# A two-block transformer kernel on one core: the feed-forward up projections in seven block products instead of eight, and one token product moved ahead of the attention logits

## The reference, cut to what matters

```python
def conv_ffn(hn, w_up, conv_w, conv_b, w_down):
    u = depthwise_conv_centred(hn @ w_up, conv_w, conv_b)     # 3 taps over the tokens
    gate, val = jnp.split(u, 2, axis=-1)
    return (jax.nn.gelu(gate, approximate=True) * val) @ w_down

def second_block(x, ...):
    for l in range(DEPTH_2):                                  # 2 layers
        mixed = hybrid_mixer(rms_norm(x, mix_pre_g[l]), ...)  # attention + mLSTM
        x = x + rms_norm(mixed, mix_post_g[l])
        ff = conv_ffn(rms_norm(x, ffn_pre_g[l]), w_up[l], ffn_conv_w[l], ffn_conv_b[l], w_down[l])
        x = x + rms_norm(ff, ffn_post_g[l])
    return x
```

## Time and profile before

| what | value |
|---|---|
| median of three executions | 2045.03 us (2043.11 to 2045.64) |
| the profiled execution: its time | 2044.89 us |
| the profiled execution: span of the trace | 2043.2 us |
| mean granted clock of TensorE | 0.989 of full speed |
| PE busy | 1953.8 us (96%), 9008 instructions |
| DVE busy | 652.7 us (32%) |
| ACT busy | 411.7 us (20%) |
| POOL busy | 110.3 us (5%) |

### The profile page before, as it was taken

The page is one execution under the profiler, slowest core; times in us unless marked ns, Lnnn a source line. Parts: engine busy times, 40 slices in busy tenths (PEclk is TensorE's granted clock), DMA queues, the critical chain, the costliest instruction groups (busy, mean ns, idle before and its releaser), DMA issues.

```text
span 2043.2 us, 23068 instructions
## 1 busy us (share of the span) xinstructions
PE 1953.8 (96%) x9008; PEld 1117.3 (55%) x9008; DVE 652.7 (32%) x1324; ACT 411.7 (20%) x871; POOL 110.3 (5%) x183
## 2 busy tenths in 40 slices
PE   7999999999989899989899999999999999999998
PEld 3767875333333233333333333756888456768863
DVE  1487513222112122211212221543333445433353
ACT  2134213111111011111101112143221023421210
POOL 0000000000000000000000000110000011000000
PEclk9999999999999999999999999999999999999999
DMA  9855368999999999999999999153544434344440
GB/s 344 295 202 191 131 231 333 418 427 428 428 427 428 428 428 427 428 428 427 428 428 428 427 426 369 62 206 114 174 137 164 147 131 165 113 135 154 136 173 33
DMA packets 136421, 582.21 MB, mean 285 GB/s; under 512 B 9848, under 2 KB 56064, under 8 KB 110752
## 3 DMA queue, kind: packets, MB, share of 16 engines
q1 hardware_dynamic: 131808, 574.70, 70.7%
q0 software_dynamic: 4544, 6.57, 1.1%
HBM read 580.18 MB, written 2.63 MB: 285 GB/s over the span
## 4 chain that ended last, share of the span: by engine, by line
PE 75%; DMA 20%; DVE 3%; ACT 1%; issue 1%; SPq 0%; DVEq 0%; ACTq 0%
PE psum L358 51%; DMA ring<-w_gu 11%; PE psum L694 11%; PE psum L636 9%; DMA work<-w_gu 9%; PE psum L2213 1%; DVE work L1854 1%; PE psum L681 1%; PE psum L670 1%; PE psum L1078 1%; DMA ring<-w_ada 0%; PE psum L1120 0%; PE psum L1109 0%; SPq L461 0%; DVE work L1852 0%
## 5 line engine op out<-in xcount | busy, mean ns | idle before, releaser
L358 PE MATMUL psum<-normed,ring 128*128 128x256 f32 (+1 forms) x2400 | 497.1, 368 | 0.0
L358 PEld LDWEIGHTS psum<-normed,ring 128*128 128x128 f32 x2400 | 434.4, 190 | 58.3 <-issue 4.1
L636 PE MATMUL psum<-ring,normed 128*64 128x512 f32 x1024 | 236.3, 615 | 33.0 <-DMA ring<-w_gu 31.8
L636 PE MATMUL psum<-work,normed 128*64 128x512 f32 x1024 | 234.3, 612 | 29.3 <-DMA work<-w_gu 29.3
L358 PE MATMUL psum<-work 128*128 128x128 f32 (+7 forms) x1248 | 227.3, 352 | 1.9 <-ACT work L2554 1.7
L358 PEld LDWEIGHTS psum<-work 128*128 128x128 f32 (+2 forms) x1248 | 151.7, 185 | 87.3 <-issue 74.3
L358 PE MATMUL psum<-ring,work 128*128 128x512 f32 (+1 forms) x464 | 197.5, 578 | 0.1
L636 PEld LDWEIGHTS psum<-ring,normed 128*64 128x64 f32 x1024 | 76.0, 141 | 190.9 <-issue 164.3
L636 PEld LDWEIGHTS psum<-work,normed 128*64 128x64 f32 x1024 | 80.5, 141 | 181.1 <-issue 181.1
L358 PE MATMUL psum<-ring,normed 128*128 128x512 f32 (+1 forms) x368 | 152.3, 567 | 0.7 <-PE psum L358 0.4
L358 PEld LDWEIGHTS psum<-ring,work 128*128 128x128 f32 x464 | 87.4, 190 | 100.0 <-issue 98.7
(11 more groups left out here) (328 smaller groups left out, 1425.0 us busy)
## 6 DMA issues: line engine op xcount, KB each, us to landing
ring<-w_gu SPq DMA_DIRECT2D x64, 2048.0 KB, 27.3
work<-w_gu SPq DMA_DIRECT2D x62, 2048.0 KB, 27.3
work<-w_dn SPq DMA_DIRECT2D x32, 2048.0 KB, 27.2
ring<-w_dn SPq DMA_DIRECT2D x28, 2048.0 KB, 27.5
ring<-w_in SPq DMA_DIRECT2D x23, 2048.0 KB, 10.1
ring<-w_up SPq DMA_DIRECT2D x44, 1024.0 KB, 7.2
ring<-w_down SPq DMA_DIRECT2D x10, 2048.0 KB, 7.8
ring<-w_ada SPq DMA_DIRECT2D x8, 2048.0 KB, 9.0
```

What stands on the lines that cost most here:

```text
L358: return pe.matmul(out, lhsT, rhs, start=first, stop=last, **kw)
L636: ins = pe.matmul(b[r], self.hgT[:, 2 * q + k, r], ws[e][:, k, n0:n0 + 512], start=q == 0 and k == 0, stop=q == QUARTERS - 1 and k == 1, s ...
```

## The change: what it does

1. **Seven products for eight in the up projections** (chunks 2 to 21 of both layers, `up_sevens`). For a chunk, the weights are seen as two parts (gate, value) by two halves of each pair of feature blocks, the tokens as two halves of each pair by two token tiles. Seven products of sums of these blocks, each summed over four pairs, replace the eight plain ones: 28 matmuls with 128 moving columns instead of 16 with 256. Four of the seven go to one PSUM bank (`up`), three to another (`upb`).
2. **Sums of the weights on POOL**: four instructions of 512 columns for every chunk (lines 2214 to 2217 of the changed kernel), the second of them written back into the ring slot. They wait for the chunk two places ahead to be done on the PE, since their results have two buffers.
3. **Sums of the tokens on DVE**: four instructions of 512 columns once a layer, behind the second tile's norm.
4. **Totals on DVE and ACT** for every chunk: ACT copies the first product out of PSUM (`first_product`, 128 columns), DVE makes four sums of one PSUM operand and one SBUF operand (`up_totals`, 256, 256, 128 and 256 columns), into a buffer `u_out` in SBUF. Both banks are released there. ACT's taps and DVE's outer taps then read `u_out` and no longer PSUM.
5. **The order on DVE and ACT is skewed**: in step c DVE does the totals of chunk c, the outer taps of c-1 and the product of c-2.
6. **The sums of hidden chunks** for the down projection move from POOL to DVE, behind steps 10 and 18.
7. **In the mixing stage**, PE's value product of tile 1 moves in front of the logits of tile 0, and the list of PSUM banks follows.

The core of the diff:

```diff
-    u += [("S", l, 0, g) for g in range(4)] + [("mv", l, 1)] + [("S", l, 1, g) for g in range(4)]
+    u += [("mv", l, 1)] + [("S", l, t, g) for t in range(NT) for g in range(4)]
...
-    u += [("up", l, c) for c in range(2, FC)]
+    u += [(name, l, c) for c in range(2, FC) for name in ("upb", "up")]
...
+    x_sums = Arena(mem.work, xn_at).take(4, KC // 2, P)
+    u_sums = [Arena(mem.work, at).take(4, P) for at in (aqk_at + 4096, aqk_at + 4608, hid_at + FC * L, ex_at + 1536, ex_at + 2048, ex_at + 2560)]
+    u_sums = [u_sums[0:3], u_sums[3:6]]
+    u_out = [hm.rearrange("p t h n -> p (t h) n"), mem.gain.rearrange("p (a b) -> p a b", b=P)]
...
+    def up_of(l, c, part):
+
+        if c < 2:
+            return bank("up", l, c)[:, part * L:(part + 1) * L]
+        return u_out[c % 2].rearrange("p a b -> p (a b)")[:, P + 4 * P * part:P + 4 * P * part + L]
...
-            for g in range(SEVENS // 4):
-                pool.wait_ge(hid_ready, l * FC + 8 * g + 8)
-                pairs = hid[:, 8 * g:8 * g + 8].rearrange("p (i k) t -> p i k t", k=2)
-                a11, a12, a21, a22 = (pairs[:, :, k, t * P:(t + 1) * P] for t in range(2) for k in range(2))
-                s1, s2, s3, s4 = (s_sums[:, i, 4 * g:4 * g + 4] for i in range(4))
+            for c in range(2, FC):
+                if c == 2:
+                    pool.wait_ge(*B.ready("O", l, 1))
+                elif c >= 4:
+                    pool.wait_ge(*B.ready("up", l, c - 2))
+                if c == 5 and l + 1 < LAYERS:
+                    pool.wait_ge(gain_used, (2 * l + 1) * 2)
+                    gain_rows(l + 1, 0)
+                if c % 2 == 0:
+                    pool.wait_ge(*S.ready("up", l, c // 2))
+                w = slot(S.no(("up", l, c // 2)), KC, 512).rearrange("p (i k) n -> p i k n", k=2)
+                a11, a12, a21, a22 = (w[:, :, k, 256 * part + P * (c % 2):256 * part + P * (c % 2) + P] for part in range(2) for k in range(2))
+                s1, s2, s4 = u_sums[c % 2]
                 step(pool.tensor_tensor(s1, a21, a22, ALU.add))
-                step(pool.tensor_tensor(s3, a11, a21, ALU.subtract))
+                step(pool.tensor_tensor(a21, a11, a21, ALU.subtract))
                 step(pool.tensor_tensor(s2, s1, a11, ALU.subtract))
-                pool.tensor_tensor(s4, a12, s2, ALU.subtract).then_inc(s_ready, 1)
+                pool.tensor_tensor(s4, a12, s2, ALU.subtract).then_inc(rope_ready, 1)
...
+            pe.wait_ge(*up_sums_done(l, c))
+            if c == 2:
+                pe.wait_ge(s_ready, l * DOWN_SUMS + 1)
+            empty(*b)
+            empty(*a)
+            for i in range(KC // 2):
+                k, k1 = 2 * i, 2 * i + 1
+                last = i == KC // 2 - 1
+                product(b, 2, w[:, k, val], x3[:, i], i, True)
+                product(b, 1, s1[:, i], x1[:, i], i)
+                ins = product(b, 0, w[:, k1, val], x4[:, i], i)
+                if last:
+                    ins.then_inc(*B.fills(*b))
+                product(a, 1, s2[:, i], x2[:, i], i, True)
+                product(a, 3, s4[:, i], h[:, k1, P:], i)
+                product(a, 0, w[:, k, gate], h[:, k, 0:P], i)
+                ins = product(a, 2, w[:, k1, gate], h[:, k1, 0:P], i)
+            ins.then_inc(*B.fills(*a))
...
-                empty("up", l, c)
-                for part in range(2):
-                    ins = up_part(l, c, part, slice(0, L), range(KC), w)
-                ins.then_inc(*B.fills("up", l, c))
+                up_sevens(l, c, w)
...
+            by_token("mv", l, 1, 5)
             logits(l, 0)
-            by_token("mv", l, 1, 5)
             logits(l, 1)
...
+                if c < 2:
+                    act.wait_ge(*B.ready("up", l, c))
+                else:
+                    act.wait_ge(*B.released("up", l, c))
+                    act.wait_ge(*B.released("upb", l, c))
...
+            def first_product(c):
+
+                act.wait_ge(*B.ready("up", l, c))
+                act.activation(u_out[c % 2][:, 7], bank("up", l, c)[:, 0:P], ACT.Copy).then_inc(tap_ready, 1)
...
+                if c >= 2:
+                    first_product(c)
+                    gelu(c - 2)
                 tap(c)
-                if c >= 1:
-                    gelu(c - 1)
...
+            step(TT(x1, b12, b11, ALU.subtract))
+            step(TT(x3, b22, b12, ALU.subtract))
+            step(TT(x2, b22, x1, ALU.subtract))
+            TT(x4, b21, x2, ALU.subtract).then_inc(s_ready, 1)
...
-                    u, v = bank("up", l, c)[:, part * L:(part + 1) * L], taps[:, c % 3, part]
+                    u, v = up_of(l, c, part), taps[:, c % 3, part]
...
+            def up_totals(c):
+
+                filled("upb", l, c)
+                dve.wait_ge(*taps_of(l, c, True))
+                v, a, b = u_out[c % 2], cut(bank("up", l, c), 4), cut(bank("upb", l, c), 4)
+                twice = lambda n: across(v[:, n], 2)
+                step(TT(v[:, 0:2], a[:, 1:3], twice(7), ALU.add))
+                step(TT(v[:, 3:5], b[:, 1:3], twice(0), ALU.add))
+                take(TT(v[:, 2], a[:, 3], v[:, 3], ALU.add), "up", l, c)
+                take(TT(v[:, 5:7], b[:, 0:2], twice(4), ALU.add), "upb", l, c)
...
-            for c in range(FC):
-                outer_taps(c)
-                if c >= 1:
-                    hidden(c - 1)
+            for c in range(FC + 2):
+                if 2 <= c < FC:
+                    up_totals(c)
+                if 1 <= c <= FC:
+                    outer_taps(c - 1)
+                if c >= 2:
+                    hidden(c - 2)
+                if c in (10, 18):
+                    chunk_sums((c - 10) // 8)
```

More of the change, by code:

```diff
@@ L281 @@
 SEVENS = 8
+DOWN_SUMS = 1 + SEVENS // 4
 def layer_slots(l):
@@ L2113, in bank, with rope_done, up_sums_done, taps_of @@
         return psum[:, B.no(name)]
-    kinds = ("mix", "down")
+    def up_of(l, c, part):
+        if c < 2:
+            return bank("up", l, c)[:, part * L:(part + 1) * L]
+        return u_out[c % 2].rearrange("p a b -> p (a b)")[:, P + 4 * P * part:P + 4 * P * part + L]
+    def rope_done(l, n):
+        return rope_ready, l * (2 * NT + FC - 2) + n
+    def up_sums_done(l, c):
+        return rope_done(l, 2 * NT + c - 1)
+    def taps_of(l, c, first=False):
+        return tap_ready, l * (2 * FC - 2) + (c + 1 if c < 2 else 2 * c - (1 if first else 0))
     def sync(sp):
@@ L2396, in up_part, with up_sevens, product @@
             return ins
+        def up_sevens(l, c, w):
+            a, b = ("up", l, c), ("upb", l, c)
+            s1, s2, s4 = u_sums[c % 2]
+            x1, x2, x3, x4 = (x_sums[:, n] for n in range(4))
+            gate, val = slice(P * (c % 2), P * (c % 2) + P), slice(256 + P * (c % 2), 256 + P * (c % 2) + P)
+            def product(name, n, lhsT, rhs, i, fresh=False):
+                return pe.matmul(bank(*name)[:, n * P:(n + 1) * P], lhsT, rhs, start=fresh and i == 0, stop=i == KC // 2 - 1,
+                                 skip_group_check=True)
+            pe.wait_ge(*up_sums_done(l, c))
[16 more added lines that the diff above has]
+            ins.then_inc(*B.fills(*a))
         def up(l):
@@ L2953, in outer_taps, with chunk_sums @@
                         step(ins)
-                take(ins, "up", l, c)
+                if c < 2:
+                    take(ins, "up", l, c)
+                else:
+                    step(ins)
                 dve.nop().then_inc(conv2_ready, 1)
+            def up_totals(c):
[7 more added lines that the diff above has]
+                take(TT(v[:, 5:7], b[:, 0:2], twice(4), ALU.add), "upb", l, c)
+            def chunk_sums(g):
+                pairs = hid[:, 8 * g:8 * g + 8].rearrange("p (i k) t -> p i k t", k=2)
+                a11, a12, a21, a22 = (pairs[:, :, k, t * P:(t + 1) * P] for t in range(2) for k in range(2))
+                s1, s2, s3, s4 = (s_sums[:, i, 4 * g:4 * g + 4] for i in range(4))
+                step(TT(s1, a21, a22, ALU.add))
+                step(TT(s3, a11, a21, ALU.subtract))
+                step(TT(s2, s1, a11, ALU.subtract))
+                TT(s4, a12, s2, ALU.subtract).then_inc(s_ready, 1)
             def hidden(c):
```

19 lines of the change are left out of this document (9 added, 10 removed).

## The result

| | us | runs |
|---|---|---|
| before | 2045.34 median (2043.11 to 2045.71) | 4 |
| changed kernel | 2062.36 median (2061.41 to 2062.66) | 4 |
| ratio | 1.0085, 95% interval 1.0067 to 1.0102 | |
| forecast | 2016.9 (range 2014 to 2063) | |
| the rival "POOL and DVE hold each other up" | 2057 or 2089 | |

The kernel is slower by 17 us where I forecast 28 less. The profiled execution took 2061.41 us, its span is 2059.7.

A forecast was written before the change was run, and what follows sets the result against it. PE was taken to bound the kernel, busy 1953.8 of 2043.2 us. From 2044.9 us, 26.0 came off for the up-projection chunks and 2.0 for the mixing stage, giving 2016.9 us; range 2014 to 2063 for 8 in 10.

The forecast's parts named there:

- POOL and DVE hold each other up: Up projections: POOL additions and two-SBUF-operand DVE instructions exclude each other; 2057 us at 50 us hold a layer, 2089 at 66; chance 0.50.
- Term 1: Up projections: 40 chunks each shortened on PE from 6.90 to 6.25 us, -26.0 us if nothing else holds PE.
- Term 2: Mixing stage: PE's wait for ACT's copy before the logits goes, -1.0 us a layer, -2.0 us in all.
- POOL's sums ... Cost nothing; the cover is PE's own chunk: Up projections: POOL's four additions, 5.4 us a chunk, end some 0.7 us early behind PE's 6.25 us chunk.
- The outer taps stay at 0.52 each: Up projections, DVE: the four outer taps of a chunk keep their length, 2.07 us in all.
- DVE's load in a chunk: Up projections: DVE's totals 1.73 us, outer taps 2.07 and product 0.46, together 4.3 of PE's 6.25 us.
- free passage: Up projections: POOL's additions and DVE's two-SBUF-operand instructions run side by side without delay; chance 0.50.
- holding: Up projections: a DVE tap waits for POOL's addition, 0.93 or 1.23 us each, 54 a layer; chance 0.50, of which 0.39 slower.
- below 30 nothing shows: Up projections: under 30 us of DVE waiting for POOL a layer costs no time; break-even with the old kernel at 43.
- strict form (2089): Up projections: the later of two contending DVE and POOL instructions waits until the first is done, 66 us a layer; about 0.12.
- Wrong: Up projections, signs against the forecast: DVE taps 1 us or more apart or long, POOL additions stretched 0.4 us, PE waiting for sums.

## Why the prediction was wrong

**What the range was worth.** The measured 2062.36 lies just inside the range of 2014 to 2063, and only because the range took in the rival; the forecast itself had the sign wrong.

**Term 1 was right.** 28 matmuls of 128 columns at 0.223 are 6.25 us, and without the hold the chunks come every 6.25 us. PE's busy time goes from 1953.8 to 1928.3 without POOL's sums: -25.5 for the forecast -26.0. The whole forecast, 2016.9, is what the kernel takes without POOL's additions (2016.6).

**Term 2 was right.** -2.0 forecast; alone it gave -3.0 (-4.1 to -0.4 by the ratio's interval), and the wait for ACT is gone. ACT's second round of exponentials now waits 0.57 us for DVE, where 0.1 was forecast, and PE doesn't wait for it.

**The step that failed** is "POOL's sums ... Cost nothing; the cover is PE's own chunk". PE's chunk does cover POOL: it waits 0.6 us for it in two layers. But the price fell on DVE. With it failed the line "The outer taps stay at 0.52 each" (0.48 and the gap); they took 0.83 to 1.03 without the gap. DVE's load in a chunk was put at 4.3 of 6.25 us; with the measured means (taps 3.84, product 0.80) and the forecast's totals and gaps (1.73 and 0.20) it is 6.6, over PE's pace.

**The choice that failed** is that of free passage over holding, 0.50 against 0.50, settled for free passage by one row: 0.15 us in which a DVE addition ran beside the tail of a POOL instruction without getting longer. That reading was true and said nothing. The changed kernel has the like (DVE L2919 at 1730.98, 1.23 us, beside POOL's L2199 until 1731.12), and five unheld taps that start in an addition's last 0.18 us, beside 110 held taps and products. A held tap ends 0.28 us after POOL's instruction and takes 0.48 alone, so some 0.2 us at the end of POOL's instruction hold nothing; 0.15 lies within that. A short meeting at the end of an instruction couldn't tell the two cases apart, and I had no other, so I ought not to have let it choose.

**The rival was right in mechanism and nearly in size.** It gave 2057 with 50 us of hold a layer and 2089 with 66; measured were 49 and 2062.4. That the sum of the holds came out so near is in part luck: it was 54 of 0.93 us a layer, and there are 58 of 0.85. It put the end of the sevens 143 + 50 = 193 us after the start of chunk 2, and it is 195.8 in layer 0 (1445.43 to 1641.25). The 2.2 us of lower clock behind PE's long wait would make most of the difference; the formula left them out. It also let PE wait for weight sum 2, where PE in fact waits for chunk 19's totals and weight sum 0. Its "below 30 nothing shows" is refuted by the run with half of POOL's sums. And it priced the exclusion for DVE alone. POOL's additions are held as well, though by less than the 0.4 us named as a sign: 99 of the 160 start with 0.2 us or more of a two-operand DVE instruction to go, and these take 1.33 to 1.65 us; the other 61 take 1.26 to 1.29.

The Trainium skill, "SBUF — State Buffer", section "Who interferes with whom", says that a DVE instruction with two SBUF inputs contends with a GpSimd instruction that reads SBUF, not with one that only writes it, and that one with at most one SBUF input, outside the 2-port perf modes, doesn't contend. The runs agree on all three: taps from SBUF 0.83 to 1.03 us, beside fills 0.484, taps from PSUM 0.483. I gave its strict form (2089) the smaller part of the chance, and the traces bear that out: a held tap ends 0.28 us after POOL's addition, less than the 0.48 it takes alone, so it doesn't pay for the whole of the rest. The rule's plain form deserved more than half.

**The signs** named under "Wrong" were seen but for two: POOL wasn't stretched by 0.4 (0.06 in half of the additions, 0.38 at most), and PE hardly waited for `rope_ready`. Only the lengthened taps and the late weight sums came, with late totals before them, and they were enough.

## What to carry to other kernels

- Before work is moved to POOL, list what DVE runs at the same time with both operands in SBUF, and cost each such instruction at up to the length of a POOL instruction more (here up to 1.04 us for additions of 1.27). Where one operand can stay in PSUM the hold is gone; here that, with the banks of the last two chunks given back early and a sum moved out of the tightest step, turned +0.85% into -1.3%.
- A lag of a supporting engine isn't paid from its average idle time but from what it has to spare between the place of the lag and the next engine that waits for it. Look at the steps with extra work first.
- Count a long wait of PE with more than its length, for the matmuls at the lower clock behind it (here 2.2 us behind 8.3).

## What the runs showed of the hardware

- A DVE instruction with two SBUF inputs that starts with 0.26 us or more of a POOL addition to go ends 0.28 us after that addition, in all 110 taps and products of the changed kernel that do so, and is booked as one long instruction (up to 1.52 us for 0.48): in a profile this looks like a slow instruction, with no wait before it.
- The hold goes both ways. A POOL addition that starts while such a DVE instruction has 0.20 us to go takes 1.33 us for 1.27, and one that starts with 0.47 to go takes 1.60: it grows with what is left of the DVE instruction. DVE's taps are short, so POOL pays little (0.04 to 0.08 us in the mean) and the taps much (0.35 to 0.54). A long DVE stream against short POOL instructions wasn't tried.
- The granted clock was 0.50 while PE waited 8.3 us (it had fallen about 1 us before, behind a wait of 3.2), 0.62 in the mean of the 5.7 us of work behind it, then 1.00.
